# Attention keys projected already transposed, their shared rotated part turned once, and a head group's first queries projected at the end of the group ahead

## What is computed

```
z = h @ w_in;  cq, ckv, kr = z[..., :384], z[..., 384:640], z[..., 640:]
q  = (rmsnorm(cq, q_norm)   @ w_uq ).reshape(B, L, 16, 96)
kv = (rmsnorm(ckv, kv_norm) @ w_ukv).reshape(B, L, 16, 128)
q_nope, q_rope = q[..., :64], q[..., 64:]
k_nope, v      = kv[..., :64], kv[..., 64:]
q_rope, kr = apply_rope(q_rope, cos, sin), apply_rope(kr, cos, sin)   # latent tokens only
k_rope = broadcast(kr over the 16 heads)                              # one for all heads
s = q @ k.T * 96**-0.5;  p = softmax(s);  o = p @ v                   # 512 queries, 768 keys
```

## Time and profile before

| | us |
|---|---|
| median of 3 runs | 1825.88 |
| lowest, highest | 1822.14, 1827.18 |
| the profiled execution | 1821.75 |
| its span, first to last instruction | 1820.0 |
| TensorE busy | 1671.9 (92%) |
| TensorE's mean granted clock | 0.983 |
| attention's four groups, 995.4 to 1265.4 in the trace | 270.0 |

### The profile page before, as it was taken

The page is one execution under the profiler, slowest core; times in us unless marked ns, Lnnn a source line. Parts: engine busy times, 40 slices in busy tenths (PEclk is TensorE's granted clock), DMA queues, the critical chain, the costliest instruction groups (busy, mean ns, idle before and its releaser), DMA issues. The chain is left out here.

```text
span 1820.0 us, 23918 instructions
## 1 busy us (share of the span) xinstructions
PE 1671.9 (92%) x9793; PEld 871.5 (48%) x9793; DVE 709.0 (39%) x1421; ACT 529.1 (29%) x893; POOL 180.9 (10%) x198
## 2 busy tenths in 40 slices
PE   4999989799999999999998999999969998888887
PEld 2667768443333333333367878878733332222222
DVE  4667765611221221221246665666541222122123
ACT  4777883300110111111154435436210000000002
POOL 1000010010010010010011324324000000000001
PEclk8999999999999999999999999999979999999999
DMA  9554361799999999999981000001599999999996
GB/s 360 197 209 165 120 245 66 280 345 405 405 404 386 405 401 386 404 402 388 413 320 71 1 1 0 0 0 62 204 353 421 421 420 421 421 421 421 421 421 255
DMA packets 89577, 520.56 MB, mean 286 GB/s; under 512 B 11347, under 2 KB 19648, under 8 KB 33936
## 3 DMA queue, kind: packets, MB, share of 16 engines
q1 hardware_dynamic: 80128, 487.74, 66.4%
q0 software_dynamic: 9360, 31.54, 5.6%
HBM read 502.37 MB, written 16.88 MB: 285 GB/s over the span
## 5 line engine op out<-in xcount | busy, mean ns | idle before, releaser
L917 PE MATMUL wide<-sb_ring_x,sb_xT 128*64 128x512 f32 x1160 | 264.9, 598 | 19.6 <-DMA sb_ring_x<-moe_w_up 18.3
L917 PE MATMUL wide<-sb_ring,sb_xT 128*64 128x512 f32 x888 | 202.1, 597 | 12.9 <-DMA sb_ring<-moe_w_up 12.8
L917 PEld LDWEIGHTS wide<-sb_ring_x,sb_xT 128*64 128x64 f32 x1160 | 77.6, 136 | 188.6 <-issue 135.0
L917 PEld LDWEIGHTS wide<-sb_ring,sb_xT 128*64 128x64 f32 x888 | 59.9, 136 | 143.3 <-issue 104.3
L972 PE MATMUL duo<-sb_ring_x,sb_hidT 128*64 128x512 f32 x536 | 124.3, 599 | 4.4 <-DMA sb_ring_x<-moe_w_down 4.4
L1909 DVE TENSOR_TENSOR sb_hid<-wide,sb_sg 128x512 f32<-128x512 f32 x16 | 11.1, 692 | 300.1 <-ACT sb_sg_c L1439 300.1
L2365 POOL TENSOR_TENSOR sb_prob<-sb_prob,sb_asum 128x768 f32<-128x768 f32 x64 | 93.8, 1466 | 183.1 <-DVE sb_asum L2184 183.1
L972 PE MATMUL duo<-sb_ring,sb_hidT 128*64 128x512 f32 x424 | 99.9, 601 | 7.4 <-DMA sb_ring<-moe_w_down 7.4
L1437 ACT ACTIVATE sb_sg<-wide 128x512 f32<-128x512 f32 x16 | 9.6, 597 | 328.6 <-PE wide L928 328.6
L1909 DVE TENSOR_TENSOR sb_hid<-wide,sb_hid 128x512 f32<-128x512 f32 x16 | 11.1, 691 | 227.8 <-ACT sb_hid L1437 227.8
L1437 ACT ACTIVATE sb_hid<-wide 128x512 f32<-128x512 f32 x16 | 9.6, 597 | 252.1 <-PE wide L917 252.1
(11 more groups left out here) (440 smaller groups left out, 2844.5 us busy)
## 6 DMA issues: line engine op xcount, KB each, us to landing
sb_ring_x<-moe_w_up SPq DMA_DIRECT2D x145, 1024.0 KB, 28.9
sb_ring<-moe_w_up SPq DMA_DIRECT2D x111, 1024.0 KB, 28.0
sb_ring_x<-moe_w_down SPq DMA_DIRECT2D x69, 1024.0 KB, 27.7
sb_ring<-moe_w_down SPq DMA_DIRECT2D x59, 1024.0 KB, 28.1
sb_ring<-ada_w SPq DMA_DIRECT2D x40, 1024.0 KB, 6.6
sb_ring<-lru_w_in SPq DMA_DIRECT2D x8, 1024.0 KB, 9.1
sb_ring_x<-ada_w SPq DMA_DIRECT2D x8, 1024.0 KB, 13.5
sb_ring<-lru_w_out SPq DMA_DIRECT2D x4, 1024.0 KB, 6.4
```

The costliest lines, as they stand in the source:

```text
L917: ins = mm(wide[n * CAPL:(n + 1) * CAPL, s, :], mine[:, k, :], w[:, at:at + BANK], start=k == 0, stop=k == KD - 1)
```

## The change

- `k_project(j)` now makes keys transposed: the weight of one head (128x64) is stationary and `ckvT` moves, so a head's 64 plain features come out on 64 partitions, two heads side by side in `duo` bank 1. Four jobs a group: each pair of heads, with 512 latent and then with 256 context tokens. There is no `ktok`, no copy by DVE and no turn of keys; ACT and DVE make `k_hi` and `k_lo` from the bank, 64 partitions at a time.
- The rotated key goes into `krope` (128 wide, zeros in the gaps, the 32 elements twice); it is turned once by six turns into `wide`, and ACT and DVE place it in `k_hi` and `k_lo` ahead of and in the first group. Queries get the same layout in `qtok`, 128 wide instead of 96, with two half-size operations for each one that wrote the rotated part.
- `q_project(g + 1, 0)` and its `q_tile` stand in the last three units of group g. `turn_queries(0)` is then the first work of a group.
- v0 and v1 go to `wide` banks 2 and 3, and `k_project(3)` behind them.
- The loops over groups are written out on all four engines.

```diff
+            pe.wait_ge(s_krr, 7 * TLT + 1)
+            for t in range(TT):
+                ins = turn(wide[:, t // 4, t % 4 * P:(t % 4 + 1) * P], krope[:, t, :])
+            ins.then_inc(s_krt, 1)
             pe.wait_ge(s_cqT, TT)
-            with pe.Fori(0, NG) as g:
+            for g in range(NG):
...
+                def k_project(j):
+
+                    pe.wait_ge(*((s_kT, g * 4 + (j + 1)) if j else (s_OT, g * 2 + 2)))
+                    pair, cols_, n = key_job(j)
                     for k in range(KKV):
-                        w = ring_at(("ukv", k))[:, bass.ds(g * BANK, BANK)].rearrange("p (h n) -> p h n", h=HG)[:, :, 0:NOPE]
-                        ins = mm(duo[:, bank_of["k", t], 0:HG * NOPE], ckvT[:, k, t * P:(t + 1) * P], w, start=k == 0, stop=k == KKV - 1)
+                        for h in range(2):
+                            at = (g * HG + 2 * pair + h) * (NOPE + VD)
+                            w = ring_at(("ukv", k))[:, at:at + NOPE]
+                            ins = mm(duo[h * NOPE:(h + 1) * NOPE, 1, 0:n], w, ckvT[:, k, cols_], start=k == 0, stop=k == KKV - 1)
                     ins.then_inc(s_kv, 1)
...
-                def turn_keys(t):
...
+                def q_project(g, t, ks=range(KQ)):
+
+                    if ks[0] == 0:
+                        pe.wait_ge(*((s_qtok, g * 4 + (t + 2)) if t else (s_OT, g * 2 + 1)))
...
+                if g == 0:
+                    q_project(0, 0)
+                turn_queries(0)
+                for t in range(1, TLT):
+                    q_project(g, t)
+                    k_project(t - 1)
+                    turn_queries(t)
+                v_project(0)
                 v_project(1)
-                pe.wait_ge(s_kT, g * 6 + 7)
-
+                k_project(TLT - 1)
+                pe.wait_ge(s_krl, 3)
...
+                    if u == U and g < NG - 1:
+                        q_project(g + 1, 0, range(1))
+                    if u == U + 2 and g < NG - 1:
+                        q_project(g + 1, 0, range(1, KQ))
...
+            act.wait_ge(s_krt, 1)
+            rope_rows = wide[:, 0:2, :].rearrange("p a n -> p (a n)")[:, 0:T]
+            for h in range(2):
+                rows_ = slice(NOPE, P) if h == 0 else slice(0, NOPE)
+                ins = fn(k_hi[rows_, h:HG:2, :], rope_rows[rows_].unsqueeze(1).to_broadcast([NOPE, 2, T]), ACT.Copy)
+            ins.then_inc(s_krl, 1)
...
+                    pair, cols_, n = key_job(t)
+                    act.wait_ge(s_kv, g * 4 + (t + 1))
+                    for h in range(2):
+                        rows_ = slice(h * NOPE, (h + 1) * NOPE)
+                        fn(k_hi[rows_, 2 * pair + h, cols_], duo[rows_, 1, 0:n], ACT.Copy).then_inc(s_khi, 1)
+                if g == 0:
+                    act.wait_ge(s_krl, 3)
+                    for h in range(2):
+                        rows_ = slice(NOPE, P) if h == 0 else slice(0, NOPE)
+                        ins = fn(k_lo[rows_, 2 + h, :], k_lo[rows_, h, :].bitcast(F32), ACT.Copy)
+                    ins.then_inc(s_krl, 1)
...
+            v.memset(qtok[:].rearrange("p a h n -> p (a h n)").rearrange("p (a b n) -> p a b n", a=4, b=4)[:, :, 1:3, ROPE:NOPE], 0.0)
...
-                    for o, a_, b_, op in rest:
-                        ins = v.tensor_tensor(o, a_, b_, op)
+                    for o, (_, a_, b_, op) in enumerate(rest):
+                        for pair in range(2):
+                            heads = slice(2 * pair, 2 * pair + 2)
+                            half = q_tok[:, pair, 1:3, 0:ROPE].rearrange("p b (a h f) -> p b a h f", a=2, h=2)[:, :, :, o, :]
+                            ins = v.tensor_tensor(half, a_[:, heads], b_[:, heads], op)
...
+                for t in range(1, TLT):
+                    q_tile(g, t)
+                    q_rest(t - 1)
+                    k_rest(t - 1)
+                    if g == 0 and t < 3:
+                        turned_rest(t - 1)
+                v_tile(0)
                 v_tile(1)
+                q_rest(TLT - 1)
+                k_rest(TLT - 1)
...
+                if g < NG - 1:
+                    q_tile(g + 1, 0)
                 pair_out(1)
```

More of the change, by code:

```diff
@@ L272, in build @@
         mla_keep = ExitStack()
-        cqT, ckvT, krr, ropes, rtmp = [sb(n, s, F32, mla_keep) for n, s in (
+        cqT, ckvT, _, ropes, rtmp = [sb(n, s, F32, mla_keep) for n, s in (
             ("cqT", [P, KQ, TL]), ("ckvT", [P, KKV, T]), ("krr", [P, TT, ROPE]), ("ropes", [P, TLT, 2, 2 * FQ]),
@@ L353, in build @@
             "s_mz", "s_mzs", "s_cqn", "s_cqtr", "s_cqT", "s_qhi", "s_khi")]
[L354 to L355 removed]
+        s_q, s_qtok, s_qtr, s_qT, s_kv, s_krt, s_krl, s_kT = [sem(n) for n in (
+            "s_q", "s_qtok", "s_qtr", "s_qT", "s_kv", "s_krt", "s_krl", "s_kT")]
         s_S, s_max, s_exp, s_pn, s_ptr, s_PTd, s_PTa, s_av, s_OT, s_rs = [sem(n) for n in (
@@ L418, in out_lhs, with key_job, v_bank @@
             return Y[:, :, tile], Y_hi[:, t % 2], Y_lo[:, :, tile]
-        PROJECT = [("q", 0), ("k", 0), ("k", 1), ("q", 1), ("k", 2), ("k", 3), ("q", 2), ("k", 4), ("k", 5), ("q", 3)]
-        bank_of = {item: i % 2 for i, item in enumerate(PROJECT)}
+        assert HG == 4 and TLT == 4 and NOPE == 64 and ROPE == 32
+        def key_job(j):
+            pair, part = divmod(j, 2)
+            cols_ = slice(0, TL) if part == 0 else slice(TL, T)
+            return pair, cols_, cols_.stop - cols_.start
+        def v_bank(t):
+            return wide[:, 2 + t, 0:HG * VD] if t < 2 else duo[:, t % 2, 0:HG * VD]
         W0 = [2 * KD, 4 * KD]
@@ L2351, in _ @@
             pool.dma_start(ropes[:], rope.rearrange("(t p) i f -> p t i f", p=P)).then_inc(s_rope, 16)
+            g_.memset(krope[:], 0.0).then_inc(s_krr, 1)
             pool.wait_ge(s_rope, 16)
@@ L2355, in _ @@
                 if t >= 1:
-                    pool.wait_ge(s_krr, 6 * t)
-                _, rest = turn_angles(g_, krr[:, t:t + 1, :], kraw[:, t % 2:t % 2 + 1, :], 1, t, s_krr)
-                pool.wait_ge(s_krr, 6 * t + 4)
+                    pool.wait_ge(s_krr, 7 * t + 1)
+                _, rest = turn_angles(g_, krope[:, t:t + 1, 0:ROPE], kraw[:, t % 2:t % 2 + 1, :], 1, t, s_krr)
+                pool.wait_ge(s_krr, 7 * t + 5)
                 for o, a_, b_, op in rest:
                     g_.tensor_tensor(o, a_, b_, op).then_inc(s_krr, 1)
-            with pool.Fori(0, NG) as g:
+                pool.wait_ge(s_krr, 7 * t + 7)
+                g_.tensor_copy(krope[:, t, NOPE:NOPE + ROPE], krope[:, t, 0:ROPE]).then_inc(s_krr, 1)
+            for g in range(NG):
                 for u in range(HG * TLT):
```

166 lines of the change are left out of this document (58 added, 108 removed).

## The result

The changed kernel takes 1808.47 us (median of four runs, 1807.42 to 1811.66), the one before 1826.36 us beside it (four runs, 1822.14 to 1827.18): a ratio of 0.9914, interval 0.9899 to 0.9930, some 15.7 us less. A second comparison on another occasion gave 0.9912 (0.9887 to 0.9938). The forecast was 12.8 us less, 1813.1, which is the small end of that interval (12.8 to 18.4 us).

What follows compares the result with a forecast made beforehand. Attention's end starts the expert stream; TensorE bounds attention's projection stage. Three groups -13.7, first group +0.4, clock +0.5 give -12.8 us: 1825.88 to 1813.1 us, range 1807 to 1821.

Steps and rivals of the forecast that it cites:

- Rival C: Expert stream starts by something other than w_uq's release, so attention's saved time doesn't reach the end: 1826 us; 3%.
- A regular group: Projection stage, first turn to first scores, 16.28 us against 21.31; net of the seam 4.58 us less, for three groups.
- The seam: Between groups, the next group's first query projection partly fills free TensorE time and pushes the last turn by 0.45 us.
- The key job: Key products on TensorE: 1.95 us for 512 tokens, 1.1 for 256, with 0.2 for change of form; 64-wide products pair.
- Rival A: Key products don't pair and run one after the other: 18 us more, kernel at 1831 us; 4%.
- The hand-over: Query tile from projection through DVE to turn: 1.9 us, with DVE's four half-size operations at 0.57 us.
- VectorE and ACT keep up: In the projection stage their key work ends before TensorE needs it, with margins of 0.3, 1 and 0.1 us.
- rival B: Key chain on ACT and DVE is late, key jobs wait: 12% for 1817 to 1822 us, 4% for no change.
- The first group: Start to first scores 21.6 us, 0.9 less, but first exponential later by 1.3: together 0.4 us more.
- The clock, +0.5: At attention's start, a pause behind q0 may keep TensorE at lower clock: 0 to 4 us, taken as 0.5.
- rival D: The start eats more, low clock throughout it and the table load with its drain: 1818 us; 12%.
- The loops "at nothing": Writing out the loops over groups was costed at nothing, since no loop operation showed as idle time at a seam.

Runs made afterwards that it cites:

- x1: The kernel before with only the four loops over head groups written out; 1820.40 us, ratio 0.9971 to the kernel before.
- x3: The changed kernel without its seam: first queries projected at the group's own start; 1819.58 us, ratio 0.9976 to the kernel before.
- x2: x1 plus the next group's first query projection in the last units and its turn ahead of the keys, old key layout; 1816.31 us, ratio 0.9947.
- x4: The changed kernel with a key job's products in another order, both of one head and then both of the other; 1807.5 us, one timed run.
- x11: x3 with one value projection put between a group's first query projection and its turn; 1819.3 us, one timed run.
- x7: The changed kernel with early table load, later k_lo copies, a value projection behind the 256-token key job, last key job in another bank; 1804.19 us, ratio 0.9892.
- x5: The changed kernel with one tiny exponential on ScalarE ahead of attention, so the table loads in idle time; 1810.7 us, one timed run.

## Why the prediction was right, and where it wasn't

**Mechanism.** The end of attention starts the stream, one for one. Right. Before, x1, x3 and after have A of 271.0, 268.6, 266.0 and 256.4 and medians of 1826.4, 1820.4, 1819.6 and 1808.5; T varies by 4 us over all kernels, A by 20. Rival C falls.

**A regular group, -4.58.** Measured 67.20 to 62.44, -4.76. From the first turn to the first scores 16.39 us for 16.28; the three steps read off the rows above (turn to turn, twice, and the last turn to the first scores; the forecast's last two steps are one here) are 4.39 (forecast 4.35), 4.27 (4.30) and 7.73 (4.35 + 3.28 = 7.63). The seam, from the first of the four end turns (1058.15; before, 1122.28 in the earlier trace rows) to the next group's beginning (1067.29; before, 1131.03 by the earlier trace rows), takes 9.14 instead of 8.75 us, 0.39 more for 0.45 forecast. Not foreseen is 0.2 us in the scores stage (36.29 to 36.08 us), which the forecast took as unchanged. In x3 it is 36.09 too and in x1 and x2 36.24, so nearly all of it comes with the keys' layout (0.05 with the loops) and none with the seam.

**The key job.** 1.87 us start to start for 512 tokens (1.95 forecast), 1.02 to 1.03 for 256 (1.1). A job of eight instructions is thus 0.12 us above the 1.75 of the expert's products, where 0.2 was taken for the change of form. Size right, reason wrong: the prediction had two products of different heads stream side by side, and x4 shows no need of that. Rival A rested on the same pairing; no loss of its kind was seen. (The values products that it cites take 1.46/24 = 0.061 us each from start to start; its 0.064 uses the length of the row.)

**The hand-over.** VectorE's four operations took 0.50 us (0.57 forecast), the whole hand-over 1.75 us (1.9 forecast; from 1074.20, where k1 follows the projection, to the turn at 1075.95), and TensorE waits 0.67 us behind a 256-token job, about 0.8 forecast; bare, it waits 1.57 us, in the start and in x3. Right, and so is its place: in the new order no other job leaves it open.

**VectorE and ACT keep up.** Right in the changed kernel. The margin put at 0.1 us for k3 is 0.12 (x11), and x11 shows the rival B at work as soon as the stage is pulled tighter. x7 shows the next one behind it, the first maximum.

**The first group.** From q0 to the first scores 21.36 us (21.6 forecast; 22.54 before). The sum is right because two misses cancel. Up to the first turn it took 4.57 us where projection and hand-over were put at 3.20 + 1.9 = 5.1 (the forecast's memset of 0.25 lies ahead of q0 and isn't in the 21.36). From there it took 16.79 instead of 16.28, mostly because one of VectorE's two rests of the rotated key does not lie in a gap, as the forecast had it, but ahead of the third query tile:
```profile
1009.58 0.95 DVE L2170 TENSOR_TENSOR sb_k_lo<-wide,sb_k_hi 64x768 fp32r<-64x768 f32 x1
```
TensorE's wait for that tile is 1.07 us there and 0.67 in the later groups. The exponential is 3.94 us behind the scores (3.8 forecast); the stage grows by 1.1 (1.3 forecast), and x5 shows that it is the table load. The forecast had that right.

**The clock, +0.5.** In all nine traces with the new key layout the second query projection took 2.10 us, its full speed, so 0 would have been right, and rival D's part of the clock didn't come about. The fear was not baseless: in x2, with the old keys and a bare hand-over behind a slow q0 of 4.18 us, the next eight key products took
```profile
1002.95 3.01 PE L1104 MATMUL duo<-sb_ring,sb_ckvT 128*128 128x256 f32 x8
```
where the same row of the second group has 1.99. Whether q0 itself is slow is chance, with the new keys at least; when it is, it took 3.41 to 4.20 us in the four traces with the old keys, and 2.96 to 3.08 in five of the six with the new ones (3.87 in x11). The six turns ahead of it may be what helps; no run tests that.

**The loops "at nothing".** This sentence is wrong. Written out by themselves they give 0.78 us a group, 3.1 us in all. It didn't spoil the sum, because that compared a whole new group with the whole old one: most of the loops' part (0.57 of 0.78) sat in the 2.2 us of waits for query tiles, of which 1.4 were counted as going. It spoiled the account. Taken in the order loops, keys, seam, the 4.76 us a group are 0.78, 0.75 and 3.22; with the seam ahead of the keys (x1, x2, after) the loops are 0.78, the seam 1.73 and the keys 2.24. What the parts give depends on the order, since 1.5 us come only with both. The prediction listed what goes (turns 2.6, a projection 1.9, waits 1.4) without asking which edit takes it away, and under the seam's name it has only the cost of 0.45; x3 shows that without the seam a group would have saved 1.5 us instead of 4.8, and the kernel some 4 us (ratio 0.9976) instead of 16.

**The sum.** Over attention the forecast's terms were -12.8, and A measured -14.65. Of the 1.85 between them 1.7 can be placed: 0.5 from three groups, 0.2 from the last group's scores, 0.3 from the first group up to its scores (the projection itself was 0.4 faster than in before, the third query tile's wait 0.4 longer than foreseen), 0.2 from the exponential, 0.5 from the clock term. The remaining 1 us between A and the 15.7 of the ratio lies within the ratio's interval (12.8 to 18.4). That the forecast is within 3 us is in part luck: the loops' cost was inside a difference that was taken whole, and the pairing had the right price for a reason that x4 refutes.

## What to carry to other kernels

Where a step waits for another engine's answer, ask what stands between request and use: a reordering that saves instructions may uncover that wait, and a second edit that covers it can be worth more than the first; test the parts alone and together. A stage that is pulled tighter hands the bound to a queue that had tenths to spare (here VectorE's key rests and its first maximum, and ACT's table load), so write down the margins, not only the sums. Compare kernels by a pitch inside the trace when the chance at start and end is as large as the effect.

## What the runs showed of the hardware

A float32 product with 64 stationary columns and 512 moving ones took 1.87/8 = 0.234 us, one with 128 stationary columns and 256 moving ones 0.86/4 = 0.215 us: so per moving column the narrow one took 0.46 ns and the wide one 0.84, and the narrow one did so whether its neighbour wrote the same half of the bank or the other (x4). In a hardware loop the hand-offs between TensorE and VectorE that were compared were 0.07 and 0.09 us longer than with the loop written out (x1). TensorE's down-projection products followed each other every 0.24 us at a granted clock of 0.50 and every 0.13 us at 1.00 (after, before). And the table load cost its 1.28 us and no more (x5).
